# A hybrid state-space and mixture-of-experts layer: scan pairs in another order, low parts made by GpSimd, mixing spread between the last tiles

## The chip, the cores and the metric

One core of one Trainium2 chip runs the whole kernel as one program. The metric is device time in microseconds (us), from three runs. The profile is of one further execution. TensorE (PE in the rows, PEld for its weight loads), VectorE (DVE), ScalarE (ACT), GpSimd (POOL) and SyncE (SP, which only issues DMAs here) each run their own list of instructions in order and wait for one another on semaphores.

## The reference

One decoder layer is computed for 320 tokens (256 of a prompt, 8 samples of 8) with 1024 channels:

```python
hn = rmsnorm(x, norm_mix); proj = hn @ w_in
z, xbc, dt_raw, uv, gates = jnp.split(proj, [...], axis=-1)
conv = conv_b + sum(xpad[:, k:k + l] * conv_w[k] for k in range(4)); xbc_act = silu(conv)
y_ssd, new_ssm = ssd_chunked(xs, dt, a_log, b_ssm, c_ssm, ssm_init)     # the scan: 32 heads of 64, state 128, chunks of 128
y_ssd = rmsnorm((y_ssd + d_skip * xs) * silu(z), gnorm_w)
u, v = split(gelu(uv)); v = layernorm(v); y_mlp = u * (w_spatial @ v + b_spatial)
merged = sigmoid(g_ssd) * (y_ssd @ w_branch_ssd) + sigmoid(g_mlp) * (y_mlp @ w_branch_mlp)
h = x + merged @ w_out
h = h + moe_ffn(rmsnorm(h))                                             # top 4 of 32 experts; then the final rmsnorm
```

## The kernel before

The time has two large parts. Up to about 640 us runs the mixer (projection, scan, branches, output); after it the 32 experts, in pairs, whose weights stream in from memory. The change is in the first 450 us.

**Tiles.** `hn` is turned by TensorE into `hnT` (8 transposes of 3 pieces), and every projection tile is 128 output channels by 320 tokens. Weights and activations are each cut into a high part and a rest ("low part"), so that three products of reduced-precision matmuls make one full product: for a tile `q`, ScalarE casts the weights to the high part (`split_tile` on ScalarE, counted by `split_hi`), VectorE subtracts it from the weights (`split_tile` on VectorE, `split_lo`), and TensorE runs 24 matmuls in two halves of 12 (`half_tile`), lines 827 to 836. The tile that is split is always four ahead of the one just read.

**Stages.** First the `dt` tile and the eight `v` tiles, then four `z` tiles and six `conv` tiles, then the eight mixing products (`mix`, with VectorE's `add_mix_bias` behind each) and the last rows of the convolution state (`last_rows`, read by ScalarE's `read_rows`). Then comes the scan: 16 pairs of heads, `for j in range(PAIRS)` on every engine. Four pairs share a group of the state-space inputs. Beside the scan's own small matmuls each pair `j` carries the two or three projection tiles that `beside(j)` names: three in the first and second pair of a group, two in the third and fourth. In groups 1 to 3 they are six `conv` and four `z` tiles, in the last group `u` tiles and two halves of the gates.

**One pair, before, on TensorE:** `heads` (into PSUM banks 3 and 4), `turn_state` half 0, `diagonal` of the pair before, the first half-tile, in the third and fourth pair of a group `last_rows` (bank 2), `turn_state` half 1, `chunk_states`, `turn_x` of the next pair (bank 2 too), a half-tile, `new_state` and `off_diagonal` half 0, a half-tile, `new_state` and `off_diagonal` half 1, and the last half-tiles. `new_state` half 0 waits for ScalarE's second `read_state`, `new_state` half 1 for VectorE's first `sample_states`, since all use bank 7.

**On the others:** ScalarE reads the heads (`read_heads`, an exponential), copies states (`read_state`), makes `exp(seg)` (`exponent`), reads tiles (`read_beside`) and splits high parts. VectorE runs `segments`, which waits for `read_heads`, then convolutions (`convolve`, six instructions), `gated` (the output of the pair before), `weigh` (operands of the next pair), `sample_states`, and splits low parts. GpSimd multiplies the decays (`decay`), squares the outputs (`squares`) and packs convolution rows (`pack_of`). Each engine's order is the written order; nothing reorders it.

Of the kernel before, what the change touches and what calls it, by code (L numbers as in the profile page):

```python
# [20 lines left out]
P = 128  # L21
# [96 lines left out]
def build(nc, x_prompt, x_sample, state_conv, state_ssm, norm_mix, w_in, conv_w, conv_b, dt_bias, a_log,  # L118
# [4 lines left out]
    with ctx:  # L123
# [352 lines left out]
        MIX_BANKS = (5, 6, 3, 7)  # L476
        BRANCH = ([("mlp", 0), ("w", 2)] + [("y", i) for i in range(4)]
# [106 lines left out]
        def _(pool):  # L584
# [221 lines left out]
        def _(pe):  # L806
# [48 lines left out]
            for k in range(KD):  # L855
                if k >= 4:
                    pe.wait_ge(S["hnT_ready"], k - 3)
                for c in range(3):
                    mm = turn(bank[(2, 3, 6, 7)[k % 4]][:, tok(c)], hn[0:rows(c), c, k * P:k * P + P])
# [27 lines left out]
            for m in range(3, 8):  # L887
                project("v", m)
                turn_v(m - 1)
            project("z", 0)  # L890
# [5 lines left out]

            pe.wait_ge(S["dt_w"], 1)
            for kind, src in enumerate((0, None, 3, 4)):
                for c in range(3 if kind < 3 else 1):
                    v = acumT[0:H, tok(c)] if src is None else dtmp[0:H, src, tok(c)]  # L900
                    mm = turn(bank[4][0:rows(c), kind * 96 + c * H:kind * 96 + c * H + H], v)
            mm.then_inc(S["tm_psum"], 1)
            project("conv", 4)
            project("conv", 5)
# [11 lines left out]
            def last_rows(g, part):  # L916
# [3 lines left out]
                for i in range(count):  # L920
                    mm = turn(bank[2][0:STATE_ROWS, i * P:i * P + P], pack[:, first + i, :])
# [3 lines left out]
            pe.wait_ge(S["ws_ready"], 2)  # L925
            last_rows(0, 0)
            pe.wait_ge(S["v_ready"], 3)
# [4 lines left out]
            for g in range(4, GH):  # L932
                mix(g)

            def gate_half(m, i):
# [5 lines left out]
                if i == 0:  # L941
# [3 lines left out]
                    else:  # L945
                        pe.wait_ge(S["seg_ready"], PAIRS)
# [47 lines left out]
            def heads(j):  # L994

                if j:
                    pe.wait_ge(S["seg_ready"], j)
# [76 lines left out]
            for j in range(PAIRS):  # L1074
# [17 lines left out]
                if j + 1 < PAIRS:  # L1092
                    if jj >= 2 and after_g < G:
# [1462 lines left out]
```

## Time and profile before

| | us |
|---|---|
| median of the three runs (1637.15, 1639.44, 1639.19) | 1639.19 |
| the profiled execution's own time | 1635.9 |
| its span, first to last instruction | 1634.1 |
| TensorE busy in the span | 1492.4 (91%) |
| VectorE, ScalarE, GpSimd busy | 609.4, 372.9, 206.2 |
| the stretch of the 16 scan pairs, 115.9 to 449.2 | 333.3 |

How to read it: a row of the table of stretches gives the stretch, its length, each engine's busy time with its number of instructions, the granted TensorE clock as a share of full speed, the DMA share and GB/s. A timeline row gives start, duration, engine, line, operation, tiles, shape and count, and in brackets how long the engine was idle before it and who ended that. `arena` is one large on-chip buffer that holds most tiles of the mixer; `bank` is PSUM; `ring_r` holds the split weights. Pair `j` starts with its two matmuls of line 1002.

### The profile page before, as it was taken

To read this page: it belongs to the slowest core of one execution; us is meant where nothing else is said; L and a number is where in the kernel's file an instruction comes from. 1 tells how busy PE (TensorE), PEld (TensorE's weight loads), DVE (VectorE), ACT (ScalarE), POOL (GpSimd) and SP (SyncE) were. 2 spreads that over 40 slices of the span, in tenths; PEclk is the share of its full clock that TensorE was granted. 3 is DMA by queue.
4 is the path that set the end of the run, shared out by engine and by line. 5 is a ranking of instruction groups with operands and counts; after the bars stand their busy time and mean duration, and the time that the engine had idled before them with its cause. 6 is when DMAs were issued, how large, how long until landed. Compare 5 with 4: busy or idle time off the path is not lost.

```text
span 1634.1 us, 21958 instructions
## 1 busy us (share of the span) xinstructions
PE 1492.4 (91%) x8487; PEld 877.9 (54%) x8488; DVE 609.4 (37%) x1335; ACT 372.9 (23%) x626; POOL 206.2 (13%) x303
## 2 busy tenths in 40 slices
PE   5999898989999999999999998997899899999986
PEld 4988777878799964443443443443244334434432
DVE  4785676675574414221221221311231212212213
ACT  4554545454353315100100100100011001001002
POOL 4022232323275000000000000000000000000000
PEclk9998988899899999999999999998999999999998
DMA  6532433434354473999999999999699999999994
GB/s 211 155 110 82 125 117 107 135 107 135 100 153 154 155 275 142 429 427 428 429 428 428 428 429 430 427 428 421 277 428 429 430 428 428 429 429 430 428 427 183
DMA packets 123471, 495.85 MB, mean 303 GB/s; under 512 B 7205, under 2 KB 95325, under 8 KB 98009
## 3 DMA queue, kind: packets, MB, share of 16 engines
q1 hardware_dynamic: 85216, 471.74, 71.0%
q10 hardware_dynamic: 35888, 18.88, 4.0%
q0 software_dynamic: 2304, 4.40, 0.9%
q8 instruction: 40, 0.66, 0.2%
q14 instruction: 23, 0.18, 0.0%
HBM read 483.65 MB, written 11.34 MB: 303 GB/s over the span
## 4 chain that ended last, share of the span: by engine, by line
PE 57%; DMA 27%; DVE 7%; issue 5%; ACT 2%; SPq 1%; POOL 1%; ACTq 0%; DVEq 0%; POOLq 0%
DMA ring_b<-in_w_gu 26%; PE bank L1306 16%; PE bank L1359 9%; PE bank L1145 6%; PE bank L827 3%; PE bank L836 3%; PE bank L1259 3%; PE bank L1056 2%; PE bank L1067 2%; PE bank L832 2%; PE bank L1160 2%; PE bank L829 2%; PE bank L808 1%; DVE arena L2131 1%; DMA ring<-in_w_in 1%
## 5 line engine op out<-in xcount | busy, mean ns | idle before, releaser
L1306 PE MATMUL bank<-ring_b,xe 128*64 128x512 f32 x1280 | 353.3, 618 | 43.2 <-DMA ring_b<-in_w_gu 43.2
L1306 PEld LDWEIGHTS bank<-ring_b,xe 128*64 128x64 f32 x1280 | 116.7, 142 | 264.1 <-issue 263.7
L1306 PE MATMUL bank<-ring,xe 128*64 128x512 f32 x768 | 226.0, 594 | 5.7 <-DMA ring<-in_w_gu 5.5
L1359 PE MATMUL bank<-ring,actT 128*64 128x512 f32 x768 | 228.8, 598 | 0.0
L1479 ACT ACTIVATE swi<-swi 128x256 f32<-128x256 f32 x66 | 27.4, 417 | 569.3 <-DVE swi L2352 569.3
L2352 DVE TENSOR_SCALAR swi<-bank 128x256 f32<-128x256 f32 x64 | 27.2, 425 | 340.2 <-PE bank L1306 335.1
L1145 PE MATMUL bank<-rounded,ring_r 128*128 128x320 f32 x912 | 134.3, 308 | 1.9 <-DVE ring_r L2179 1.9
L1145 PEld LDWEIGHTS bank<-rounded,ring_r 128*128 128x128 f32 x912 | 133.2, 188 | 3.1 <-DVE ring_r L2179 2.9
L782 POOL TENSOR_TENSOR kept<-take 128x256 bf16<-128x256 bf16 x15 | 9.2, 613 | 875.7 <-PE bank L1341 875.7
L1359 PE MATMUL bank<-ring_b,actT 128*64 128x512 f32 x256 | 114.5, 601 | 4.3 <-ACT actT L1831 4.3
L1306 PEld LDWEIGHTS bank<-ring,xe 128*64 128x64 f32 x768 | 75.0, 137 | 77.1 <-issue 77.1
L1359 PEld LDWEIGHTS bank<-ring,actT 128*64 128x64 f32 x768 | 69.3, 137 | 63.1 <-issue 62.8
L2370 DVE TENSOR_TENSOR hid<-hid,bank 128x512 f32<-128x512 f32 (+1 forms) x90 | 57.8, 683 | 116.4 <-PE bank L1283 116.4
L827 PE MATMUL bank<-rounded,ring_r 128*128 128x320 f32 x456 | 89.5, 343 | 0.6 <-ACT rounded L1506 0.6
L836 PE MATMUL bank<-rounded,ring_r 128*128 128x320 f32 x456 | 81.4, 323 | 0.0
L1924 DVE TENSOR_TENSOR ring_r<-ring,ring_r 128x1024 fp32r<-128x1024 f32 (+1 forms) x61 | 75.4, 1237 | 3.5 <-ACT ring_r L1499 3.4
L808 PE MATMUL bank<-ident,arena 128*128 128x128 f32 (+7 forms) x305 | 50.9, 288 | 27.8 <-DVE arena L1917 17.4
L827 PEld LDWEIGHTS bank<-rounded,ring_r 128*128 128x128 f32 x456 | 75.3, 208 | 1.8 <-DVE ring_r L1924 0.8
L836 PEld LDWEIGHTS bank<-rounded,ring_r 128*128 128x128 f32 x456 | 74.8, 202 | 0.0
L1359 PEld LDWEIGHTS bank<-ring_b,actT 128*64 128x64 f32 x256 | 34.1, 138 | 66.0 <-issue 65.9
L1499 ACT CAST ring_r<-ring 128x1024 fp32r<-128x1024 f32 (+1 forms) x61 | 63.4, 1040 | 8.2 <-DMA ring<-in_w_in 6.7
L2463 DVE SCALAR_TENSOR_TENSOR ye_lo<-bank,routing,ye_hi 128x512 fp32r<-128x512 f32 x32 | 22.6, 746 | 113.2 <-ACT ye_hi L1842 113.2
(353 smaller groups left out, 2070.2 us busy)
## 6 DMA issues: line engine op xcount, KB each, us to landing
ring_b<-in_w_gu SPq DMA_DIRECT2D x83, 2048.0 KB, 17.1
ring<-in_w_down SPq DMA_DIRECT2D x50, 2048.0 KB, 18.8
ring<-in_w_gu SPq DMA_DIRECT2D x49, 2048.0 KB, 16.8
ring<-in_w_in SPq DMA_DIRECT2D x32, 1024.0 KB, 5.4
ring_b<-in_w_down SPq DMA_DIRECT2D x16, 2048.0 KB, 14.7
arena<-in_state_ssm ACTq DMA_DIRECT2D x16, 512.0 KB, 5.0
out<-arena ACTq DMA_DIRECT2D x16, 512.0 KB, 3.6
ring<-in_w_branch_ssd SPq DMA_DIRECT2D x8, 1024.0 KB, 5.3
```

The costliest lines, as they stand in the source:

```text
L808: return pe.transpose(out, in_, ident[0:in_.shape[0], 0:in_.shape[0]])
L827: pe.matmul(o, w_h[k], hn_hi[:, k, :], start=(k == 0), stop=False)
L829: pe.matmul(o, w_l[k], hn_hi[:, k, :], start=False, stop=False)
L832: pe.matmul(o, w_l[k], hn_hi[:, k, :], start=False, stop=False)
L836: mm = pe.matmul(o, w_h[k], hn_lo[:, k, :], start=False, stop=(k == KD - 1))
L1145: mm = pe.matmul(bank[4 * m + b][:, 0:T], w[:, k, m * P:m * P + P], v[:, k0 + k, :], start=(k == 0 and which != 4 and v is x_h and w is w_ ...
L1259: mm = pe.matmul(bank[6 + k // 4][:, (k % 4) * P:(k % 4) * P + P], part[0:rows(c), c, k * P:k * P + P], chosen_rows[0:rows(c), c, :], star ...
L1306: mm = pe.matmul(bank[q][side(h), :], xe[:, j, side(h)], moe_slot(2 * i + h)[:, 2 * FF * k + 512 * q:2 * FF * k + 512 * q + 512], start=Fa ...
L1359: mm = pe.matmul(bank[4 + half][side(h), :], actT[:, f, side(h)], w[:, D * k + 512 * half:D * k + 512 * half + 512], start=False, stop=(f ...
L1499: act.copy(hi, w).then_inc(S["split_hi"], 1)
L1924: dve.tensor_tensor(lo, w, hi.bitcast(F32), ALU.subtract).then_inc(S["split_lo"], 1)
L2370: dve.tensor_tensor(hid[0:rows(c), c, hb(c, half)], hid[0:rows(c), c, hb(c, half)], bank[6 + i % 2][0:rows(c), :], ALU.add).then_inc(S["cm ...
```

## The change

The scan's order is rewritten on every engine. On TensorE `last_rows` moves behind `turn_x`, into bank 3, and `heads` waits for ScalarE's exponentials (`e_ready`). On VectorE `segments` no longer waits for `read_heads`; on ScalarE `read_heads` waits for `segments`. ScalarE reads the last tile of the pair before first, both `read_state` halves and `read_chunk_states` come ahead of the tiles and of the stores, and casts are separate from tile reads. The low parts of all tiles that are split in the scan (38) are made by GpSimd's new `split_tile`. Ahead of the scan, mixing is put between the last two `conv` tiles, the small transposes that fill `tm` and half of the statistics of `v` move into the `v` tiles, and the transposes of `hn` use six banks, not four, with one split ahead of them, not three.

```diff
 # GpSimd, in the scan
+            def split_tile(q):
+                pool.wait_ge(S["split_hi"], q + 1)
+                pool.wait_ge(S["split_lo"], q)
+                w, hi, lo = tile_of(q)
+                pool.tensor_tensor(lo, w, hi.bitcast(F32), ALU.subtract).then_inc(S["split_lo"], 1)
...
                 decay(j)
                 if j:
                     squares(j - 1)
+                    kind, n = beside(j - 1)[-1]
+                    split_tile(tile_no(kind, n) + 4)
                 for i, n in enumerate(convs):
                     if i:
                         prefix_of(n)
                     pack_of(n)
+                for kind, n in beside(j)[:-1]:
+                    if kind != "gs":
+                        split_tile(tile_no(kind, n) + 4)
 # TensorE
-                if k >= 4:
-                    pe.wait_ge(S["hnT_ready"], k - 3)
+                if k >= 6:
+                    pe.wait_ge(S["hnT_ready"], k - 5)
...
-            for g in range(4):
-                mix(g)
+            mix(0)
+            mix(1)
+            project("conv", 4)
+            mix(2)
+            mix(3)
+            project("conv", 5)
+            last_rows(0, 0)
...
             def heads(j):
                 if j:
-                    pe.wait_ge(S["seg_ready"], j)
+                    pe.wait_ge(S["e_ready"], j)
...
-                elif jj >= 2 and after_g < G:
-                    pe.wait_ge(S["xw_ready"], j + 1)
-                    last_rows(after_g, jj - 2)
...
                 if j + 1 < PAIRS:
-                    if jj >= 2 and after_g < G:
-                        pe.wait_ge(S["cs_ready"], 2 * after_g + jj - 1)
                     turn_x(j + 1)
+                if jj >= 2 and after_g < G:
+                    pe.wait_ge(S["e_ready"], j + 1)
+                    last_rows(after_g, jj - 2)
 # ScalarE
             def read_heads(j):
-                act.wait_ge(S["head_psum"], j + 1)
+                act.wait_ge(S["seg_ready"], j + 1)
...
+                if j:
+                    read_beside(late)
+                    convolved += [n for kind, n in (late,) if kind == "conv"]
+                read_state(j, 0)
                 read_heads(j)
-                read_state(j, 0)
                 exponent(j)
                 if jj == 0:
                     read_b(j // 4)
-                elif jj >= 2 and after_g < G:
+                read_state(j, 1)
+                read_chunk_states(j)
+                if jj >= 2 and after_g < G:
                     read_rows(after_g, jj - 2)
                 if j:
-                    store_states(j - 1)
+                    split_after(late)
 # VectorE
             def segments(j):
                 dve.wait_ge(S["head_psum"], j + 1)
-                dve.wait_ge(S["e_ready"], j + 1)
...
             def use(tile):
-                if kind != "gs":
-                    split_tile(tile_no(kind, n) + 4)
...
                 segments(j)
                 if j:
-                    use(beside(j - 1)[-1])
+                    gated(j - 1)
+                    use(late)
```

GpSimd, from the middle of the second pair of a group (pair 1) to the casts behind the third's decay. Lines 664 and 665 pack rows (663 and 664 in the kernel before), 686 is `decay` (685), 695 to 697 `squares` (694 to 696), 653 the prefix (652). Before:

```order
L663 COPY arena<-arena 128x3
L664 COPY arena<-arena 128x24
L652 COPY arena<-arena 128x8x3
L685 TENSOR_TENSOR arena<-arena 128x640
L694 TENSOR_TENSOR arena<-arena 128x320
L695 TENSOR_TENSOR arena<-arena 128x320
L696 TENSOR_SCALAR arena<-arena 128x320
L663 COPY arena<-arena 128x3
```

and after:

```order
L664 COPY arena<-arena 128x3
L665 COPY arena<-arena 128x24
L716 TENSOR_TENSOR ring_r<-ring,ring_r 128x8x128 x2
L653 COPY arena<-arena 128x8x3
L686 TENSOR_TENSOR arena<-arena 128x640
L695 TENSOR_TENSOR arena<-arena 128x320
L696 TENSOR_TENSOR arena<-arena 128x320
L697 TENSOR_SCALAR arena<-arena 128x320
L716 TENSOR_TENSOR ring_r<-ring,ring_r 128x8x128
L664 COPY arena<-arena 128x3
```

Two subtractions of 128 by 1024 elements now stand between the pack of the second pair's last tile and the third pair's decay, and a third one behind its squares.

ScalarE, the start of pair 2 (the third of its group). Lines 1558 and 1559 (1577 and 1578 after) and the activation of 320 behind them read a `conv` tile, 1499 (1517) is a cast to a high part, 1638 (1658) `read_state`, the 64x192 activations `read_heads`, the 128x640 one `exponent`, 1647 (1667) and 1650 (1670) `read_chunk_states`, 1586 (1606) `read_rows`. Before:

```order
L1499 CAST ring_r<-ring 128x8x128 [waits proj_ready]
L1479 ACT_TABLE_LOAD [waits off_read,sn_ready]
L1479 ACTIVATE arena<-bank 64x192 [waits head_psum]
L1479 ACTIVATE arena<-bank 64x192
L1638 COPY arena<-bank 128x512 [waits off_psum,sT_psum]
L1479 ACTIVATE arena<-arena 128x640 [waits yd_psum,seg_ready]
L1586 COPY arena<-bank 27x512 [waits cs_psum]
...
L1479 ACT_TABLE_LOAD
L1479 ACTIVATE arena<-arena 128x320 [waits conv_done]
L1638 COPY arena<-bank 128x512 [waits off_psum,sT_psum]
```

and after:

```order
L1577 COPY arena<-bank 128x256 [waits packed,conv_act,conv_done,proj_ready]
L1578 COPY arena<-bank 128x8x8
L1497 ACTIVATE arena<-bank,arena 128x320
L1658 COPY arena<-bank 128x512 [waits off_psum,sT_psum]
L1497 ACT_TABLE_LOAD [waits off_read,sn_ready]
L1497 ACTIVATE arena<-bank 64x192 [waits seg_ready]
L1497 ACTIVATE arena<-bank 64x192
L1497 ACTIVATE arena<-arena 128x640 [waits yd_psum,seg_ready]
L1658 COPY arena<-bank 128x512 [waits off_psum,sT_psum]
L1667 COPY arena<-bank 128x128 [waits off_psum,sf_psum]
L1670 COPY arena<-bank 128x128 [waits s_fin_out0]
L1606 COPY arena<-bank 27x512 [waits cs_psum]
```

The second `read_state` now follows the exponential directly; the cast, the row read, the stores and the silu that stood ahead of it are behind it.

## Rows read from the trace of the kernel before

**Rows 1.** Table of stretches: the scan, then pairs 9 to 14.

```profile
115.90:449.20 333.30, 310.70 (x1849) 258.41 (x1848) 208.98 (x527) 159.03 (x287) 103.14 (x133) 0.90 0.37 111
...
313.30:334.60 21.30, 20.24 (x127) 17.51 (x126) 13.26 (x32) 10.53 (x18) 5.68 (x7) 0.92 0.33 103
334.60:352.60 18.00, 15.96 (x106) 12.74 (x105) 13.72 (x37) 10.65 (x20) 5.76 (x10) 1.00 0.41 121
352.60:371.00 18.40, 15.79 (x104) 12.56 (x103) 12.39 (x33) 9.39 (x17) 6.12 (x6) 1.00 0.40 118
371.00:391.30 20.30, 20.09 (x136) 16.93 (x135) 12.91 (x30) 9.90 (x17) 8.59 (x9) 1.00 0.55 164
391.30:418.50 27.20, 24.86 (x126) 21.29 (x125) 12.69 (x29) 9.48 (x15) 5.93 (x4) 0.75 0.29 80
418.50:434.00 15.50, 15.34 (x102) 12.37 (x101) 10.35 (x27) 8.21 (x13) 6.62 (x4) 1.00 0.46 141
```

**Rows 2.** TensorE's waits in the scan: us in total, times, longest.

```profile
PE bank L1056 <- ACT arena L1638: 10.8, 10, 2.3
PE bank L808 <- ACT arena L1586: 3.1, 3, 1.0
PE bank L1056 <- DVE arena L2143: 3.0, 2, 1.5
PE bank L808 <- ACT arena L1638: 2.8, 8, 0.5
PE bank L808 <- ACT arena L1589: 2.5, 3, 0.8
```

**Rows 3.** Timeline of TensorE in pair 10: start, us, then the instructions.

```profile
334.57 0.55 PE L1002 MATMUL bank<-rounded,rounded 64*128 64x320 f32 x2
...
344.62 1.09 PE L1056 MATMUL bank<-arena 32*128 32x512 f32 x2 [0.70 <-ACT arena L1638]
...
348.72 1.12 PE L1056 MATMUL bank<-arena 32*128 32x512 f32 x2
```

**Rows 4.** Timeline of ScalarE in pair 10: the second read of the state.

```profile
343.91 0.57 ACT L1638 COPY arena<-bank 128x512 f32<-128x512 f32 x1
```

**Rows 5.** Timeline of VectorE in pair 10.

```profile
338.68 1.51 DVE L2131 TENSOR_SCALAR arena<-bank,arena 128x128 f32<-128x128 f32 x6 [4.06 <-issue]
...
341.22 1.57 DVE L2042 SCALAR_TENSOR_TENSOR arena<-arena 128x64 f32<-128x64 f32 x1
...
345.93 1.34 DVE L2099 TENSOR_TENSOR arena<-bank,arena 128x256 f32<-128x256 f32 x5
347.19 1.11 DVE L2143 SCALAR_TENSOR_TENSOR arena<-arena,bank 128x128 f32<-128x128 f32 x4
```

**Rows 6.** Line 2042 on VectorE alone: ns minimum, median, maximum, first and last start.

```profile
L2042 DVE SCALAR_TENSOR_TENSOR arena<-arena x54: 269/279/1585, 125.6 to 361.3; 128x64 f32<-128x64 f32 x54
```

**Rows 7.** Lines 685 and 695 on GpSimd alone, the same columns.

```profile
L685 POOL TENSOR_TENSOR arena<-arena x16: 1548/1672/2100, 123.8 to 439.9; 128x640 f32<-128x640 f32 x16
...
L695 POOL TENSOR_TENSOR arena<-arena x15: 858/872/2810, 175.1 to 455.1; 128x320 f32<-128x320 f32 x15
```

**Rows 8.** Groups by line: busy us, mean ns of one, idle before.

```profile
L749 POOL TENSOR_TENSOR arena<-arena,bgu_parts 32x512 f32<-32x512 f32 x4 | 6.7, 1677 | 0.3
```

**Rows 9.** Timeline of TensorE at its start.

```profile
23.10 3.83 PE L808 MATMUL bank<-ident,arena 128*128 128x128 f32 x12 [1.97 <-DVE rounded L1930]
27.55 2.47 PE L827 MATMUL bank<-rounded,ring_r 128*128 128x320 f32 x8 [0.61 <-ACT rounded L1506]
```

**Rows 10.** Timeline of VectorE ahead of the scan.

```profile
103.31 0.38 DVE L2064 MEMSET arena<- 128x384 f32 x1
...
104.59 0.48 DVE L2040 SCALAR_TENSOR_TENSOR arena<-arena 128x256 f32<-128x256 f32 x1 [0.26 <-ACT arena L1479]
...
115.20 0.42 DVE L2076 TENSOR_TENSOR arena<-bank,arena 128x256 f32<-128x256 f32 x1 [0.95 <-PE bank L913]
```

**Rows 11.** The page's DMA issues: operation, count, KB each, us to landing.

```profile
arena<-in_state_ssm ACTq DMA_DIRECT2D x16, 512.0 KB, 5.0
```

More of the change, by code:

```diff
@@ L889, in _ @@
                 turn_v(m - 1)
+                if m == 6:
+                    pe.wait_ge(S["dt_w"], 1)
+                    for kind, src in enumerate((0, None, 3, 4)):
+                        for c in range(3 if kind < 3 else 1):
+                            v = acumT[0:H, tok(c)] if src is None else dtmp[0:H, src, tok(c)]
+                            mm = turn(bank[4][0:rows(c), kind * 96 + c * H:kind * 96 + c * H + H], v)
+                    mm.then_inc(S["tm_psum"], 1)
             project("z", 0)
@@ L895, in _ @@
                 project("conv", n)
[L897 to L904, printed above, removed]
             def mix(g):
@@ L920, in last_rows @@
                 for i in range(count):
-                    mm = turn(bank[2][0:STATE_ROWS, i * P:i * P + P], pack[:, first + i, :])
+                    mm = turn(bank[ROWS_BANK if g else 2][0:STATE_ROWS, i * P:i * P + P], pack[:, first + i, :])
                 mm.then_inc(S["cs_psum"], 1)
@@ L1501, in _ @@
             act.wait_ge(S["ident_ready"], 1)
-            for q in range(3):
-                split_tile(q)
+            split_tile(0)
             for k in range(KD):
                 act.wait_ge(S["hnT_psum"], k + 1)
-                act.copy(hn_hi[:, k, :], bank[(2, 3, 6, 7)[k % 4]][:, 0:T]).then_inc(S["hn_hi_ready"], 1)
+                act.copy(hn_hi[:, k, :], bank[2 + k % 6][:, 0:T]).then_inc(S["hn_hi_ready"], 1)
+            for q in range(1, 3):
+                split_tile(q)
             q = tile_no("dt", 0)
@@ L1680, in read_beside, with split_after @@
                     read_u(n)
+            def split_after(tile):
+                kind, n = tile
                 if kind != "gs":
@@ L2001, in _, with half_stats @@
                               ).then_inc(S["dt_w"], 1)
+            stats = ysum[:, 0:36].rearrange("p (c n) -> p c n", c=3)
+            def half_stats(half):
+                for c in range(3):
+                    r = rows(c)
+                    i = dve.bn_stats(stats[0:r, c, 6 * half:6 * half + 6], vtok[0:r, c, hb(c, half)])
+                link(i)
             for m in range(3, 8):
@@ L2087, in _ @@
             add_mix_bias(1)
+            convolve_beside(4)
+            add_mix_bias(2)
+            add_mix_bias(3)
             convolve_beside(5)
-            for g in range(2, GH):
+            for g in range(4, GH):
                 add_mix_bias(g)
@@ L2182, in _ @@
             for j in range(PAIRS):
-                tiles = beside(j)
+                tiles, late = beside(j), beside(j - 1)[-1] if j else None
                 segments(j)
                 if j:
-                    use(beside(j - 1)[-1])
+                    gated(j - 1)
+                    use(late)
                 if j % 4 == 0:
                     mask_cb(j // 4)
-                if j:
-                    gated(j - 1)
-                if len(tiles) == 3:
-                    use(tiles[0])
                 if j + 1 < PAIRS:
@@ L2195, in _ @@
                 sample_states(j, 0)
-                if len(tiles) == 2:
-                    use(tiles[0])
+                use(tiles[0])
                 sample_states(j, 1)
```

84 lines of the change are left out of this document (46 added, 38 removed).

## The prediction

> **What bounds the kernel now.** I read four views in this order. The table of stretches first: in the 16 scan pairs TensorE is busy 310.7 of 333.3 us, so it idles 22.6, and the granted clock is 0.90 on the mean [rows 1]. VectorE is busy for 209 us of it and GpSimd for 103. So TensorE is the bound, with two losses on top: 22.6 us of idling, and 0.10 x 333.3 = 33 us of lost clock. The rows of the pairs show that these go together: pairs 10, 11, 12 and 14 ran at 1.00, pair 13 with 2.3 us of idling at 0.75 [rows 1]. Then the waits, and who ends them: ScalarE's `read_state` (line 1638) 10.8 + 2.8 us, its `read_rows` (lines 1586 and 1589) 3.1 + 2.5, and VectorE's `sample_states` (line 2143) 3.0 [rows 2]. Then the timelines of pair 10 show why. ScalarE comes to its second `read_state` only at 343.91 [rows 4], 9.3 us after the pair's start at 334.57 [rows 3], since it reads and casts tiles first; and VectorE starts `segments` 4.1 us into the pair, after 4.06 us of idling [rows 5], because `segments` waits for `read_heads`.
>
> The expert part behind 450 us has no changed instruction, and starts as soon as the mixer's last product is there. What is saved or lost ahead of it is saved or lost in full.
>
> **The floor of the scan.** A pair without waits at full clock takes: first of a group 20.3 - 0.2 = 20.1 (pair 12). Second: 21.3 - 1.06 idle (21.3 - 20.24) - 8% of 21.3 for the clock = 18.5 (pair 9). Third 18.0 - 2.04 = 16.0, fourth 18.4 - 2.61 = 15.8 (pairs 10, 11). In the last group the two-tile pairs have no row transposes: 15.5 - 0.2 = 15.3 (pair 14) [rows 1]. Three groups of 70.4 and one of 69.2 make 280.4 us, 53 below the 333.3 of now.
>
> **The start: -2.2.** TensorE waited 1.97 us between the first and the second dozen of transposes, which takes 3.83 and starts at 23.10 [rows 9]. With six banks that wait goes: the second dozen starts at 21.1 and ends at 24.9; one cast and one semaphore later, about 25.4, the first tile starts, where it started at 27.55. What hides the two weight casts moved behind, and their low parts, is that tile's own 24 matmuls (the first 8 take 2.47); were it not there, the 2.2 would be used up.
>
> **Mixing between the tiles: -2.7.** Here VectorE is the bound. The copies into `tm` and its memset stood from 103.31 to 104.33, followed by a wait of 0.26; a wait of 0.95 for TensorE came ahead of the last mixing bias [rows 10]. All go: the copies lie in gaps of the `v` tiles, and the products are there long before VectorE gets to them. That is 1.02 + 0.26 + 0.95 = 2.2; I add 0.5 for a shorter chain behind the statistics, between 0 (a square root on ScalarE hides all of it) and 1.9 (three of six statistics go). TensorE will idle longer ahead of pair 0; that costs only clock.
>
> **What a low part costs on GpSimd.** No row shows it. Nearest rows: 0.86 us for 320 elements, 1.55 to 1.67 for 640 [rows 7], so about 2.5 ns for each further one and 0.87 + 704 x 0.0025 = 2.6 us for 1024. Bounds: 640 elements at 1.548 give 2.4 ns each, 2.5 us; the subtraction of 512 elements at 1677 ns [rows 8] gives 3.3 ns each, 3.35 us. I take 2.6, since the same width of 128 partitions stands in rows 7 and not in rows 8.
>
> **What it costs VectorE.** 341.22 in pair 10: a step of the convolution that takes 0.28 us as a rule took 1.57 [rows 5, 6], just while GpSimd's 1.67 us decay ran. VectorE's instructions with one PSUM input kept their time under GpSimd's load (1.11 and 1.34 in rows 5). So a GpSimd subtraction holds up a VectorE instruction with two on-chip inputs until its end, and such a one goes in between two of GpSimd's. The Trainium skill, SBUF — State Buffer, Who interferes with whom, states this as a lock on a shared port, held for a whole instruction; the trace agrees, with the number above. The GPSIMD Engine Reference, Key points, says that VectorE is about twice as fast for elementwise work; its 2048-element figure, halved, would be 2.25 us, an estimate by which the stalls below would come out some 0.7 us a group smaller. By that page the move is a loss on the engine's side; it is one for the kernel only where GpSimd is waited for.
>
> **Pair 10 after the change**, us from its start. VectorE: `segments` 0.7 to 2.2, for it waits for the heads alone. ScalarE: late tile, `read_state`, table, `read_heads` to 3.7, `exponent` to 4.4, second `read_state` to 5.0. TensorE reaches that wait at 8: the 10.8, the two `read_rows` waits (bank 3 now, read later) and the 2.8 go. But GpSimd does two subtractions first, 1.1 to 3.7 and 4.05 to 6.65, with one of `gated`'s two instructions between and the other behind it, to 7.05. The late convolution follows, six instructions (three times 0.40 + 0.28 at their pitch, 2.0 us), interleaved with decay (1.6), the two squares of 0.7 and 0.9: done at 12.4. `weigh` (1.3) to 13.7 and `sample_states` (1.1) to 14.8. TensorE wants that at 348.72 - 334.57 - 2.04 = 12.1 [rows 1, 3]: a new wait of 2.8 in each third pair. Queued behind `sample_states` on VectorE are the next convolution and the output of the pair, for which TensorE waits only a pair later. In the fourth pair only one subtraction is ahead; the same count ends at 12.3 against 11.9: 0.4. In the first and second pair of a group `sample_states` comes before the convolutions, and TensorE has 20 and 18.5 us: no wait. The last group has no convolutions: none. The low parts themselves are in time, each by 3 us or more in this count. On ScalarE the stores, and with them the load of the state after next, move behind the copies and the cast, to about 8 to 9 us; it lands 5.0 later [rows 11], and is due at the next pair's start, at 16.
>
> Sum: 3 groups x 3.2 = 9.6 us of waits where there were 22.6. Clock: 33 us were lost with 22.6, 1.46 each; by that ratio 14. The scan takes 280.4 + 9.6 + 14 = 304, against 333.3: -29.3. All told -2.2 - 2.7 - 29.3 = -34.2, on 1635.9 of the profiled execution 1601.7. The median stands 3.3 above that execution: **1605 us**. With the bounds of the subtraction (2.5 and 3.35 us, each tenth moves a third pair by 0.2), the clock between nothing and twice the ratio's, and the start, this case spans 1592 to 1622.
>
> **The rivals.**
> *All waits go* (chance 0.14). GpSimd's instructions fall where VectorE has none with two on-chip inputs, or a subtraction takes 2.3. For it speaks that VectorE ends only 3.0 us of today's waits, in two places [rows 2]. Against it: VectorE and GpSimd already collide at 341.22. The scan is then 280 to 285: 1635.9 + 3.3 - 4.9 - 51 = about 1583.
> *The wait changes hands* (0.22). With subtractions of 3.35 us and every collision, `sample_states` comes 1.5 later in each third pair, 1 to 2 us late in each other one: 7 us a group, 21 in all with 31 of clock. The scan stays at 333, and 4.9 of the front remain: 1634, which is half within what can be told.
> *The port saturates* (slower, 0.14). The exclusive work of a group is GpSimd's four decays, eight squares, one mask (some 17 us), ten subtractions, and VectorE's six convolutions and eight steps of `gated` (16). With 2.6 us that is 59 of 70.4; with 3.7 it is the whole floor, and from about 4 on GpSimd sets the pair's time. At 10 us of waits a group: 280.4 + 30 + 44 = 354, and 1655. It decides from some 7.5 us of waits a group, a subtraction of about 3.5.
> That the change does nothing is excluded: the rows' waits have their causes in an order that is no longer there.
>
> **How the numbers follow.** Forecast 0.50, all gone 0.14, changed hands 0.22, saturated 0.14. A measurement of this kernel can tell 0.2% (3.3 us) from no change. Faster by more: 0.50 + 0.14 + half of 0.22 = 0.75. Within: 0.10. Slower: 0.15. The range leaves out half of the case in which all waits go (0.07, below 1584) and most of the saturated one (0.12, above 1637): 1584 to 1637. The forecast's own range is 1592 to 1622.
>
> **What would show it.** Right: the first tile near 25.4; pair 0 near 111; no wait left on `read_rows` or the second `read_state`; the wait of `new_state` on `sample_states` up, only in third pairs and of 2 to 3.5 us; subtractions of 2.5 to 2.9 us; convolution steps as long as those where they meet. Wrong: subtractions over 3.3, waits of a half-tile for the low part, waits in first and second pairs, or a clock as low as before in spite of fewer waits.

## The result, and the profile after

The changed kernel takes 1583.43 us (median of four runs, 1583.14 to 1589.26), the kernel before 1638.17 in the same comparison: a ratio of 0.968, 95% interval 0.965 to 0.971. That is faster by 3.2%. The forecast of 1605 us was 21.6 us too slow; the time came out where the rival "all waits go" had put it (1583). It lies outside the forecast's own range of 1592 to 1622 and right at the lower edge, 1584, of the wide one. One execution of run 6 below (1666.0 us) fell in a slower state of the core and is left out of its numbers. The profiled execution took 1583.14 us, with a span of 1581.4 where it was 1634.1.

The table of stretches of the changed kernel, in the columns of [rows 1]: ahead of the scan, the scan, the rest, and then, of a second table, pairs 1 to 4, 6, 7, 10 and 11.

```profile
0.00:112.24 112.24, 92.43 (x609) 86.16 (x610) 79.37 (x161) 59.12 (x97) 26.86 (x67) 1.00 0.57 174
112.24:396.43 284.19, 279.81 (x1847) 235.36 (x1847) 186.16 (x489) 163.22 (x288) 179.66 (x171) 0.98 0.44 130
396.43:1581.40 1184.97, 1088.63 (x6033) 533.06 (x6032) 320.41 (x648) 153.40 (x242) 75.22 (x103) 0.98 0.89 371
...
130.97:149.59 18.62, 18.62 (x127) 15.92 (x126) 10.27 (x34) 10.62 (x18) 8.97 (x13) 1.00 0.41 122
149.59:166.59 17.00, 15.61 (x107) 12.83 (x106) 16.00 (x35) 10.95 (x20) 13.22 (x13) 1.00 0.43 127
166.59:181.91 15.32, 15.32 (x105) 12.62 (x104) 11.63 (x29) 10.06 (x18) 11.98 (x10) 1.00 0.49 143
181.91:201.70 19.79, 19.79 (x136) 16.92 (x135) 13.29 (x33) 11.72 (x22) 13.04 (x13) 1.00 0.58 164
...
220.31:239.65 19.34, 17.85 (x106) 14.94 (x106) 15.69 (x35) 10.94 (x20) 12.91 (x13) 0.87 0.37 113
239.65:255.75 16.10, 16.10 (x104) 13.10 (x103) 10.26 (x29) 10.05 (x18) 11.98 (x10) 0.94 0.45 135
...
294.19:312.49 18.30, 16.80 (x106) 13.88 (x106) 15.70 (x35) 10.95 (x20) 12.93 (x13) 0.93 0.40 119
312.49:328.13 15.64, 15.64 (x104) 12.81 (x103) 11.04 (x29) 10.05 (x18) 11.82 (x9) 0.98 0.48 139
```

The scan took 333.3 us [rows 1] and takes 284.2; the scan began at 115.9 and begins at 112.2. What follows it is as long as before, 1184.97 against 1634.1 - 449.2 = 1184.9. So -3.7 and -49.1 make the whole -52.7, and what is saved ahead of the experts is saved in full, as forecast. In the scan TensorE's idling fell from 22.6 to 4.4 us, and all of it stands in the third pairs of the first three groups (17.00 - 15.61, 19.34 - 17.85 and 18.30 - 16.80). Clock is lost only in pairs 6 and 10 and in the pair behind each; pair 2 keeps 1.00 in spite of its wait: 0.13 x 19.34 + 0.06 x 16.10 + 0.07 x 18.30 + 0.02 x 15.64 = 5.1 us, where 33 were lost. GpSimd is busy for 180 us of the stretch, not 103.

TensorE's waits in the first 450 us of the changed kernel, in the columns of [rows 2]; left out are the 17.3 us ahead of its first instruction and two of 0.6 and 1.0 us outside the scan:

```profile
PE bank L1076 <- DVE arena L2183: 4.4, 3, 1.5
PE bank L1163 <- DVE ring_r L2218: 1.6, 2, 0.8
PE bank L1022 <- DVE arena L2118: 1.2, 1, 1.2
...
PE bank L821 <- ACT arena L1606: 0.6, 1, 0.6
```

Four of the five waits of [rows 2] are gone from the scan, and one is there in a new size: `new_state` on `sample_states` (line 2183 now), once in each of three third pairs. The wait of 1.2 is the one for the last mixing bias ahead of pair 0, the 1.6 are in the branch work behind the scan, and the 0.6 on `read_rows` (line 1606) stands at 108.33, ahead of the scan.

The timeline of the changed kernel in pair 2, a third pair, which began at 149.59: VectorE, then GpSimd's part of it (a second view), then TensorE and ScalarE.

```profile
150.17 1.51 DVE L2171 TENSOR_SCALAR arena<-bank,arena 128x128 f32<-128x128 f32 x6 [1.66 <-PE bank L1022]
...
152.20 1.01 DVE L2201 TENSOR_TENSOR arena<-arena 128x192 f32<-128x192 f32 x1
153.24 2.62 DVE L2203 TENSOR_TENSOR arena<-arena 128x320 f32<-128x320 f32 x1
155.78 0.48 DVE L2086 SCALAR_TENSOR_TENSOR arena<-arena 128x256 f32<-128x256 f32 x1
156.18 1.58 DVE L2088 SCALAR_TENSOR_TENSOR arena<-arena 128x64 f32<-128x64 f32 x1
...
159.88 0.47 DVE L2088 SCALAR_TENSOR_TENSOR arena<-arena 128x64 f32<-128x64 f32 x1
160.27 1.33 DVE L2140 TENSOR_TENSOR arena<-bank,arena 128x256 f32<-128x256 f32 x5
161.53 1.10 DVE L2183 SCALAR_TENSOR_TENSOR arena<-arena,bank 128x128 f32<-128x128 f32 x4
```

```profile
150.60 4.91 POOL L716 TENSOR_TENSOR ring_r<-ring,ring_r 128x1024 fp32r<-128x1024 f32 x2
...
155.88 1.79 POOL L686 TENSOR_TENSOR arena<-arena 128x640 f32<-128x640 f32 x1
...
159.45 1.38 POOL L697 TENSOR_SCALAR arena<-arena 128x320 f32<-128x320 f32 x1
```

```profile
162.69 1.12 PE L1076 MATMUL bank<-arena 32*128 32x512 f32 x2 [1.40 <-DVE arena L2183]
```

```profile
154.10 0.59 ACT L1658 COPY arena<-bank 128x512 f32<-128x512 f32 x1
```

`segments` starts 0.6 us into the pair, where it started after 4.1 in pair 10 of the kernel before [rows 3, 5], and the second `read_state` 4.5 us in, where it came after 9.3 [rows 3, 4]. The two low parts run from 150.60 to 155.51, and `gated`'s last product, usually 0.49 us, takes 2.62: it ends at 155.86, just after the second low part. Its neighbour takes 1.01 in place of 0.36. Then the convolution collides with the decay (156.18, 1.58 us for a step of 0.29), and `sample_states` is done at 162.63, 1.3 us after TensorE first wanted it (162.69 - 1.40 = 161.29). This is the mechanism that the forecast described, with the same instructions in the same places.

### The profile page after: what moved, and what is told of

The parts are those of the page before. It is cut to its first block, busy times and chain, and to the rows that moved or that the text cites. A ratio compares the mean times of both kernels' runs of the same rounds, so it can differ in the third digit from the quotient of the medians.

```text
span 1581.4 us, 22023 instructions
## 1 busy us (share of the span) xinstructions
PE 1460.9 (92%) x8487; PEld 854.6 (54%) x8488; DVE 585.9 (37%) x1297; ACT 375.7 (24%) x626; POOL 281.7 (18%) x341
## 4 chain that ended last, share of the span: by engine, by line
PE 61%; DMA 27%; DVE 7%; issue 2%; ACT 1%; SPq 1%; POOL 1%; DVEq 0%; ACTq 0%; POOLq 0%
DMA ring_b<-in_w_gu 27%; PE bank L1324 17%; PE bank L1377 9%; PE bank L1163 7%; PE bank L849 3%; PE bank L840 3%; PE bank L1277 3%; PE bank L821 3%; PE bank L1076 2%; PE bank L1178 2%; PE bank L845 2%; PE bank L1087 2%; PE bank L842 2%; PE bank L1433 1%; DVE arena L2088 1%
## 5 line engine op out<-in xcount | busy, mean ns | idle before, releaser
L1163 PE MATMUL bank<-rounded,ring_r 128*128 128x320 f32 x912 | 134.3, 308 | 1.8 <-DVE ring_r L2218 1.8
L1163 PEld LDWEIGHTS bank<-rounded,ring_r 128*128 128x128 f32 x912 | 133.2, 187 | 3.0 <-DVE ring_r L2218 2.8
L716 POOL TENSOR_TENSOR ring_r<-ring,ring_r 128x1024 fp32r<-128x1024 f32 x38 | 90.6, 2385 | 2.6 <-ACT ring_r L1517 0.6
L840 PE MATMUL bank<-rounded,ring_r 128*128 128x320 f32 x456 | 81.8, 322 | 0.6 <-ACT rounded L1523 0.6
L849 PE MATMUL bank<-rounded,ring_r 128*128 128x320 f32 x456 | 78.2, 314 | 0.0
L849 PEld LDWEIGHTS bank<-rounded,ring_r 128*128 128x128 f32 x456 | 71.4, 193 | 0.0
L840 PEld LDWEIGHTS bank<-rounded,ring_r 128*128 128x128 f32 x456 | 68.5, 191 | 2.0 <-issue 0.8
L821 PE MATMUL bank<-ident,arena 128*128 128x128 f32 (+7 forms) x305 | 48.4, 283 | 17.9 <-DVE arena L1943 17.3
```

Of the source, the lines that this page charges most:

```text
L716: pool.tensor_tensor(lo, w, hi.bitcast(F32), ALU.subtract).then_inc(S["split_lo"], 1)
L821: return pe.transpose(out, in_, ident[0:in_.shape[0], 0:in_.shape[0]])
L840: pe.matmul(o, w_h[k], hn_hi[:, k, :], start=(k == 0), stop=False)
L849: mm = pe.matmul(o, w_h[k], hn_lo[:, k, :], start=False, stop=(k == KD - 1))
L1163: mm = pe.matmul(bank[4 * m + b][:, 0:T], w[:, k, m * P:m * P + P], v[:, k0 + k, :], start=(k == 0 and which != 4 and v is x_h and w is w_ ...
```

## The experiments

All were timed in three rounds, the last two in five. The kernel before stood at 1635.5 us beside runs 1 to 4 and at 1636.3 us beside the others; ratios are to it. The changed kernel was timed only in the comparison above, beside 1638.2 us, so a difference of 2 or 3 us from its 1583.4 is no more than the kernel before moved from one comparison to the next, and smaller readings rest on the spans and the wait rows. Diffs are against the changed kernel, where nothing else is said.

**1. The low parts a pair earlier.** In each second pair GpSimd makes the low parts at once, before it waits for the convolution's halves that belong to the next pair, so that the third pair starts without them.

```diff
+                if j % 4 == 1 and convs:
+                    for kind, n in beside(j)[:-1]:
+                        if kind == "conv":
+                            pack_of(n)
+                        split_tile(tile_no(kind, n) + 4)
+                    prefix_of(convs[-1])
+                    pack_of(convs[-1])
+                    continue
```

> The changed kernel, but in the second pair of each group GpSimd makes the low parts of its first two tiles before it waits for the last tile's rows, not behind them. My theory: the three waits left in the third pairs (1.40, 1.49, 1.50 us) come from those two subtractions, since they stand at the start of the third pair and hold up the last step of gated (2.62 us where 0.49 is usual) and with it the convolution ahead of sample_states. Then the waits go, and with them the clock lost there (5 us): 9 us less than the changed kernel, near 1574. Rival: the decay and squares alone hold up the convolution enough; then a wait of 1 us or more stays in the third pairs, and the time is within 3 us of 1583. A second rival: the subtractions now collide with the convolution at the end of the second pair and make segments late: waits in new places.

Measured: 1573.7 us, ratio to before 0.962 (0.956 to 0.968), span 1572.1. The timeline of VectorE around pair 2:

```profile
148.37 2.35 DVE L2094 SCALAR_TENSOR_TENSOR arena<-arena 128x256 f32<-128x256 f32 x1
...
152.26 1.50 DVE L2179 TENSOR_SCALAR arena<-bank,arena 128x128 f32<-128x128 f32 x6
...
154.26 0.36 DVE L2209 TENSOR_TENSOR arena<-arena 128x192 f32<-128x192 f32 x1
154.65 0.49 DVE L2211 TENSOR_TENSOR arena<-arena 128x320 f32<-128x320 f32 x1
```

and of GpSimd:

```profile
148.03 2.40 POOL L716 TENSOR_TENSOR ring_r<-ring,ring_r 128x1024 fp32r<-128x1024 f32 x1 [1.07 <-ACT ring_r L1525]
```

The stall went with the subtraction: the products of `gated` are back at 0.36 and 0.49, and a convolution step at the end of pair 1 now takes 2.35 us, about as long as the subtraction beside it. `segments` starts 2.1 us later for it (152.26 in place of 150.17), and TensorE does not come to wait. No wait of `new_state` is left in the scan. The span fell by 9.3, about the 4.4 us of waits and the 5.1 of clock together. Only the place of these subtractions on GpSimd differs, so the stall's cause is shown.

**2. The low parts on VectorE again**, in the rest of the new order: GpSimd's calls are gone, and VectorE makes each behind work of its own that TensorE waits for.

```diff
                 sample_states(j, 0)
+                if j:
+                    low_of_next(late)
                 use(tiles[0])
...
                 decayed(j)
+                low_of_next(tiles[0])
```

> The changed kernel, but with the 38 low parts of the scan on VectorE (1.22 us each), each placed where its high part is there. My theory: GpSimd's share in the gain is nothing, the new order did it all: VectorE has 98 of 284 us free and the port is less used, so the waits in the third pairs vanish and the time is 1574 to 1584. Rival: VectorE needs the relief; then TensorE waits for sample_states or for the low parts in first and second pairs, over 8 us in all, and the time is 1590 to 1610.

Measured: 1572.6 us, 0.961 (0.955 to 0.967), span 1571.4. The stretch from 112 to 397 us, in the columns of [rows 1]:

```profile
112.00:397.00 285.00, 284.95 (x1920) 241.18 (x1921) 210.38 (x533) 171.77 (x295) 97.11 (x136) 1.00 0.45 135
```

TensorE idles for 0.05 us in it, at full clock, though VectorE carries 210 us of work. In this order GpSimd's part in the change brings nothing and costs about 10 us.

**3. Only the low parts moved:** the kernel before, with GpSimd's `split_tile` in the changed kernel's places and none in VectorE's `use`.

```diff
+                    kind, n = beside(j - 1)[-1]
+                    split_tile(tile_no(kind, n) + 4)
...
+                for kind, n in beside(j)[:-1]:
+                    if kind != "gs":
+                        split_tile(tile_no(kind, n) + 4)
```

> The kernel before, with only the 38 low parts moved to GpSimd. My theory: the waits of before were ScalarE's order; they stay (16 to 20 us on read_state and read_rows), and the clock stays near 0.90 in the scan: 1625 to 1650, within 0.8 percent of 1638. Rival: freeing VectorE was worth a good part of the 55 us: 1600 to 1620.

Measured: 1634.4 us, 1.001 (0.997 to 1.005). TensorE's waits in the scan:

```profile
PE bank L1068 <- ACT arena L1650: 13.4, 10, 2.7
PE bank L1068 <- DVE arena L2155: 4.7, 2, 2.4
PE bank L820 <- ACT arena L1598: 3.1, 3, 1.0
PE bank L820 <- ACT arena L1650: 2.8, 8, 0.5
PE bank L820 <- ACT arena L1601: 2.4, 3, 0.8
```

They are the five of [rows 2], 22.2 us there and 26.4 here: a relief of VectorE by 38 low parts removes none of them. With run 2 this shows that the scan's gain is the order's: the order without the move has all of it, the move without the order none.

**4. `segments` waits for the heads' readings again**, as before the change (ScalarE's own wait goes back to TensorE's heads, and TensorE's three waits on `e_ready`, not shown, to `seg_ready`).

```diff
-                act.wait_ge(S["seg_ready"], j + 1)
+                act.wait_ge(S["head_psum"], j + 1)
...
                 dve.wait_ge(S["head_psum"], j + 1)
+                dve.wait_ge(S["e_ready"], j + 1)
```

> The changed kernel, but segments waits for read_heads again, and read_heads for the heads alone, as before. My theory: VectorE starts each pair about 3 us later; in third pairs the wait on sample_states grows from 1.5 to 2 to 4 us each, elsewhere it is covered (TensorE has 3 us or more there): 3 to 8 us more waits, 6 to 15 us slower than 1583. Rival: VectorE's later start is hidden everywhere since GpSimd's two subtractions set the time in third pairs: within 3 us of 1583.

Measured: 1624.7 us, 0.992 (0.990 to 0.995), so 41 us of the change's gain are gone, where 6 to 15 had been expected. TensorE's waits, and VectorE in pair 2:

```profile
PE bank L1076 <- DVE arena L2184: 22.6, 6, 4.3
PE bank L821 <- DVE arena L2184: 2.0, 2, 1.0
```

```profile
154.78 1.51 DVE L2172 TENSOR_SCALAR arena<-bank,arena 128x128 f32<-128x128 f32 x6 [4.90 <-issue]
```

VectorE idles for 4.90 us and comes that much later to `sample_states`: 2.9 to 4.3 us of waiting in each third and fourth pair of the first three groups, and a clock of 0.91 in the stretch from 112 to 397. This run does not tell how much of it is the late start alone, and how much GpSimd's subtractions add to it; run 5 asks that.

**5. The same with the low parts on VectorE** (the edits of 2 and 4).

> segments waits for read_heads again, as in the run that cost 41 us, but the 38 low parts are made by VectorE. It asks what made that wait dear. Theory 1: the late start of VectorE alone puts sample_states behind the convolution in third and fourth pairs; VectorE has 1.2 us more to do for each tile here, so TensorE waits as much as there, 4 us a pair: 1610 to 1625. Theory 2: the late start was dear because it pushed VectorE's two-input steps under GpSimd's subtractions, decay and squares; without the 38 subtractions the waits shrink to 1 to 2 us a third pair: 1578 to 1595.

Measured: 1602.7 us, 0.980 (0.974 to 0.986). Its waits:

```profile
PE bank L1071 <- DVE arena L2179: 12.2, 6, 2.1
```

Against run 2 the late start costs 30 us (12.2 of waits, the rest clock and small waits); with GpSimd's subtractions added it costs 41 against the changed kernel, and the subtractions cost 22 here (4 against 5), where they cost 10 in the changed kernel. The two causes are not independent: both eat the same slack ahead of `sample_states`, and neither of the two ranges that were expected for this run (1610 to 1625, 1578 to 1595) was met.

**6. The second `read_state` late:** it and the chunk states are read by ScalarE behind the stores and the silus, and behind the first tile where there are three, much as before the change.

```diff
-                read_state(j, 1)
-                read_chunk_states(j)
...
                     split_after(tiles[0])
+                read_state(j, 1)
+                read_chunk_states(j)
                 read_beside(tiles[-2])
```

> The changed kernel, but ScalarE reads the second half of the states (and the chunk states) behind the first tile, the stores and the silus again. My theory: this was the largest wait of before (10.8 us with 2.8 more), so the wait of new_state on this copy is back, 1 to 3 us in most pairs, 12 to 30 us in all, with the clock: 1605 to 1640. Rival: with segments early and the casts behind, ScalarE gets there in time anyway, and the time is within 5 us of 1583.

Measured: 1643.3 us, the median of executions of 1638.7, 1643.3 and 1654.4; those of the kernel before beside it took 1627.5 to 1639.5. The expected 1605 to 1640 was passed, and the gain is gone; whether the kernel is slower than the one before, these few executions do not tell. Its span is 1636.9, against 1634.1. ScalarE in pair 2 (which starts at 152.42 here), then TensorE's waits, then the scan's row:

```profile
163.21 0.47 ACT L1497 ACTIVATE arena<-arena 128x320 f32<-128x320 f32 x1 [1.50 <-DVE arena L2088]
163.58 0.57 ACT L1658 COPY arena<-bank 128x512 f32<-128x512 f32 x1
```

```profile
PE bank L1076 <- ACT arena L1658: 22.8, 11, 4.3
```

```profile
112.93:454.27 341.34, 318.30 (x1848) 264.97 (x1848) 185.23 (x489) 161.40 (x288) 178.75 (x171) 0.86 0.37 108
```

The copy stands 11.2 us into the pair, later than the 9.3 of the kernel before, behind an activation that waits for the convolution (line 2088), which GpSimd's subtractions have held up. TensorE waits 22.8 us for it, as much as it idled in all before, and the clock is lower (0.86). So without this place in ScalarE's order the other edits bring nothing in this version. But the run does not price the place alone: part of its 60 us may be the subtractions' doing, and the same edit with the low parts on VectorE was not run. Nor do the parts add up: this run gives back 60 us and run 4 gives back 41, of a gain of 55.

**7. The rows of the convolution state as before** (bank 2, `last_rows` ahead of `turn_state` half 1, `read_rows` right behind `exponent`).

```diff
-        ROWS_BANK = 3
+        ROWS_BANK = 2
...
+                elif jj >= 2 and after_g < G:
+                    pe.wait_ge(S["xw_ready"], j + 1)
+                    last_rows(after_g, jj - 2)
```

> The changed kernel, but with the last rows of the convolution in bank 2 and ahead of turn_x again, read right behind exponent. My theory: the two waits of about 1 us on read_rows come back in third and fourth pairs of three groups, 5 to 6 us, and 3 to 8 of clock: 1589 to 1598. Rival: ScalarE is now early enough there: within 3 us of 1583.

Measured: 1585.8 us, 0.971 (0.967 to 0.975), span 1580.0 (the changed kernel's 1581.4). The waits on `read_rows` do not come back. Both kernels' intervals overlap, so the move of the rows is worth nothing that can be told here (5 to 6 us of waits had been expected back): what made TensorE wait on `read_rows` before was how late ScalarE was, not the bank.

**8. The start as before** (four banks for the turned `hn`, three splits ahead of it).

```diff
-                    mm = turn(bank[2 + k % 6][:, tok(c)], hn[0:rows(c), c, k * P:k * P + P])
+                    mm = turn(bank[(2, 3, 6, 7)[k % 4]][:, tok(c)], hn[0:rows(c), c, k * P:k * P + P])
...
-            split_tile(0)
+            for q in range(3):
+                split_tile(q)
```

> The changed kernel with the transposes of hn on four banks and three splits ahead of them, as before. Both theories: 2.2 to 2.4 us slower, 1585.5; if the scan is bound by something else than its start, less than that.

Measured: 1588.0 us, 0.971 (0.968 to 0.975). Medians cannot part it from the changed kernel; the span is 3.5 us longer (1584.9), one profiled execution each. TensorE's timeline at the start of the changed kernel, to read beside [rows 9]:

```profile
17.30 7.35 PE L821 MATMUL bank<-ident,arena 128*128 128x128 f32 x24 [17.30 <-DVE arena L1943]
25.26 2.47 PE L840 MATMUL bank<-rounded,ring_r 128*128 128x320 f32 x8 [0.61 <-ACT rounded L1523]
```

All 24 transposes run in one piece, and the first tile starts 2.29 us earlier than in [rows 9].

**9. GpSimd's work behind each low part raised** by three additions of 320 elements (3.0 to 3.1 us together; their results are not used).

```diff
+                for i in range(3):
+                    link(pool.tensor_tensor(sq, hn_hi[:, i, :].bitcast(F32), hn_hi[:, i + 3, :].bitcast(F32), ALU.add))
```

> The changed kernel with three further additions of 320 elements on GpSimd behind each of the 38 low parts (about 2.6 us more each; their result is not used). This prices the saturated port of the prediction: the two engines' exclusive work then comes to some 80 us a group of which TensorE needs 69. My theory: TensorE waits 7 to 15 us a group for sample_states and low parts and the kernel gets close to before or over it, 1620 to 1660. Rival: the lock holds up less than a whole instruction (the convolution of a third pair took 4.5 us where I had counted 5.4), and the load is hidden: 1590 to 1610.

Measured: 1617.5 us, 0.990 (0.986 to 0.993). Its waits:

```profile
PE bank L1078 <- DVE arena L2185: 13.0, 5, 3.6
PE bank L1165 <- POOL ring_r L716: 4.1, 1, 4.1
PE bank L1078 <- ACT arena L1660: 3.0, 2, 1.5
```

GpSimd is busy for 251 of the 285 us behind 112. Even so 13.0 of these 20.1 us are waits for VectorE, held up beside it, and only once, right behind the scan, does TensorE wait for a low part itself. With 2.3 times GpSimd's work for a low part the kernel loses 34 us and stays ahead of the one before; both ranges that were expected (1620 to 1660, 1590 to 1610) missed it. The saturated rival had put 1655 us at a subtraction of about 3.5 us. Here GpSimd has 5.4 us of two-input work for each low part, and the time is 1617.5: that rival counted the two engines' work as dearer than it is.

**10. The low parts only written:** two fills with zero in place of each subtraction, 1.9 us together. They read nothing; the low parts are left out of the products' values.

```diff
-                pool.tensor_tensor(lo, w, hi.bitcast(F32), ALU.subtract).then_inc(S["split_lo"], 1)
+                link(pool.memset(lo.bitcast(F32), 0.0))
+                pool.memset(lo.bitcast(F32), 0.0).then_inc(S["split_lo"], 1)
```

> The changed kernel, but in place of each of the 38 subtractions GpSimd writes zeros into the low part, twice, which takes about as long and reads nothing on chip. (It leaves the low parts of those weights out.) Lock on the reading side, as the Trainium skill has it (SBUF, Who interferes with whom): VectorE's two-input steps keep their 0.28 to 0.49 us during it, the step of gated in third pairs falls from 2.62 to 0.5 us, the three waits on sample_states go, and the time is 1572 to 1577. If any GpSimd instruction blocks VectorE: the steps stay at 1.5 to 2.6 us, the waits stay, and the time is 1581 to 1586.

Measured: 1573.0 us, 0.962 (0.956 to 0.968). VectorE's product of `gated`, and GpSimd beside it:

```profile
151.84 0.49 DVE L2204 TENSOR_TENSOR arena<-arena 128x320 f32<-128x320 f32 x1
```

```profile
151.91 0.96 POOL L716 MEMSET ring_r<- 128x1024 f32 x1
```

Both run at once and the product keeps its 0.49 us, where it took 2.62 beside a subtraction. So it is not GpSimd's being busy, nor its writing, that holds VectorE, but that its instruction reads on-chip operands.

**11 and 12. The two best orders again,** in five rounds: runs 1 and 2 as they were.

> The same kernel as in the run with GpSimd's low parts early in the second pair (1573.7 us), in more rounds, beside the one with the low parts on VectorE. My theory: 1573, as the other; if the shared load costs anything that the wait rows don't show: 2 us or more above it.

> The same kernel as in the run with the low parts on VectorE (1572.6 us), in more rounds: to tell it from the kernel in which GpSimd makes them early. My theory: neither has a wait in the scan that is left, so both take 1573 and the ratio between them is 1 within 0.2 percent. If VectorE's load matters anywhere: over 1577.

Measured: low parts a pair earlier 1574.3 us (1572.6 to 1576.3), 0.963 (0.958 to 0.967); on VectorE 1572.8 us (1571.8 to 1573.7), 0.962 (0.957 to 0.966). Both are about 10 us faster than the changed kernel. The ratios to the kernel before do not part them from its 0.968 (0.965 to 0.971), since that kernel itself scatters by over 20 us; the times do: no execution of these two orders took over 1576.7 us, and none of the changed kernel's under 1583.1. Between the two the medians differ by 1.4 us, 0.1%, too little to choose by; VectorE's version leaves GpSimd out of it.

## Why the prediction was right, and where it was off

- **What bounds it, and the chain.** Right. TensorE is the bound, the waits on `read_state` and `read_rows` had their cause in the engines' order (runs 2 and 3), and without the early `read_state` nothing is gained (run 6). Of the two reasons given for `read_rows`, the other bank was not one (run 7). What lies behind the scan kept its length.
- **The start: -2.2.** Right: -2.29, the first tile at 25.26 where 25.4 was forecast.
- **Mixing: -2.7.** Mis-sized. Of the 3.7 us ahead of the scan, 1.4 are left beside the start's. The wait of 0.95 for TensorE did go, but VectorE's list was not shorter by its whole length: VectorE has no idle time from 99.5 us on, and TensorE waits for it ahead of pair 0 (1.2 us, `L1022 <- DVE L2118`). Pair 0 starts at 112.2, not near 111. Undoing the mixing alone was not run, so the 1.4 is a difference of two readings.
- **The low part: 2.6 us.** It takes 2.39 (median of 38, 2.35 to 2.46), below the lower bound of 2.5. The line through 320 and 640 elements [rows 7] was too steep.
- **What it costs VectorE.** Right in kind: 2.62 us for a product of 0.49 and 1.01 for one of 0.36, gone when the subtraction is moved (run 1), taken off (run 2) or replaced by a write (run 10). The Trainium skill, SBUF — State Buffer, Who interferes with whom, states an exclusive lock that lasts for the whole instruction; these runs agree for GpSimd's two-input instructions, but not for its one-input operation (last section). The Trainium skill, GPSIMD Engine Reference, Elementwise — side-by-side cycle accounting, has 4497 ns for 2048 elements; half of it, 2.25 us, was an estimate for the subtraction, nearer to the 2.39 than mine. The prediction took the move for a loss only where GpSimd is waited for. That was wrong: it costs 10 us here while TensorE never waits for GpSimd in the scan, because it waits for VectorE, which GpSimd holds.
- **Pair 10 after the change: `sample_states` at 14.8, wanted at 12.1.** I had it 1.8 us too late: read in pair 2, it ends 13.0 us into the pair. Of this 0.8 had arisen when `gated` ends (6.3 in place of 7.05: shorter subtractions, and an earlier start), and 0.9 in the convolution (4.5 us, counted at 5.35). TensorE came for it at 11.7. The wait is 1.4 to 1.5, in place of 2.8; in the fourth pair there is none, in place of 0.4. So 4.4 us of waits, where 9.6 were forecast: 5.2 of the miss. The terms named for the convolution (2.0, 1.6, 0.7 and 0.9) make 5.2, not the 5.35 between 7.05 and 12.4.
- **Clock: 14 us.** The biggest miss: 5.1 were lost, 9 less. 7.6 of these follow from fewer waits at the same 1.46 (5.2 x 1.46); the rest, 1.3, from a lower price, 1.16 us for each us of wait. So the waits' size is at the root of nearly 13 of the 21.6 us. Pair 2 idled 1.40 us and kept 1.00, pair 6 idled 1.49 and fell to 0.87: a ratio taken from 22.6 us of waits is rough for three short ones. The rows had shown it: pairs 10 and 11 idled 2.04 and 2.61 us at 1.00 [rows 1], against the prediction's sentence that the two losses go together.
- **The floor: 280.4 us.** It is 284.2 - 4.4 - 5.1 = 274.7. A third pair is 15.6 without its wait and a fourth 15.3, where I had 16.0 and 15.8, second pair and first 18.6 and 19.8; pair 0, which carries no output of a pair before, takes 18.7. This is 5.7 of the miss. I took an undisturbed pair from pairs with waits, less their idle time, and that leaves a rest in: without a wait TensorE's next instructions start, by the rows, some 0.16 us before the last have ended (170.38 + 0.60 and 170.82 in pair 3 after the change), and ahead of a wait this overlap is lost and counted as busy. Pair 11 had three waits and 15.79 us of busy time [rows 1]; pair 3 after the change, also a fourth pair and without a wait, has 15.32.
- **The base.** I added 3.3 us to get from the profiled execution to the median. The kernel after shows 0.3 between the two: 3 of the miss.

The sum, then: 5.2 + 9 + 5.7 + 3 - 1.2 (ahead of the scan) = 21.7 of the 21.6. The mechanism held, and the sizes did not: of three signs set down for the forecast, the wait was 1.4 to 1.5 us and not 2 to 3.5, the subtraction 2.39 and not 2.5 to 2.9, and pair 0 came at 112.2. Nearly all sizes in the scan erred to the long side (the second pair alone was 0.1 short), so the misses added up instead of cancelling, and took the time out of the forecast's own range. The rival "all waits go" met the number, but not the way: three waits remained, and the lower floor and the smaller step to the median made up for them. That this rival's number was met is luck. "The wait changes hands" and "the port saturates" did not happen (the latter's 17 us of GpSimd's work a group are also 14 by the rows: 6.7 of decays, 6.4 of squares, 1.0 of the mask); run 9 shows that even 2.3 times the work for a low part does not bring the second about.

What stays open: how the change's parts would rank if each were undone in the best version (runs 1 and 2), what the mixing's move is worth by itself, and what the late second `read_state` costs when VectorE makes the low parts.

## What to carry to other kernels

When one engine waits for many results in a fixed order, order each helper's list by when that engine needs them: one 0.6 us copy left behind stores and silus cost 60 us here, while taking 38 instructions off the busiest helper brought nothing. Try such moves together: two of them each gave back most of the gain when undone alone. Before work is given to GpSimd, look at which VectorE instructions with on-chip operands run beside it and who waits for those; it is free only in the pairs that have slack. Count a TensorE wait at more than its length, and take the size of an undisturbed stage from a stage that shows neither waits nor a lowered clock.

## What the runs showed of the hardware

- **The clock's price of a wait varies.** All kernels in the scan: 22.6 us of idling with 33 lost before, 4.4 with 5.1 after, and in run 6 23.0 us (341.34 - 318.30) with 0.14 x 341.34 = 48. Idling cost between 1.2 and 2.1 us of clock for each us, by clock shares that the rows give to 0.01.
- **A fill does not hold up VectorE; a subtraction does.** 0.49 us under a fill of 1024 elements, 2.62 under a subtraction of the same tile. GpSimd's one-input operation of line 697 does not hold VectorE for its length either: VectorE's step at 159.88 took 0.47 beside it, not the 1.38 of GpSimd's, and in pairs 6 and 10 (230.18, 304.08) a step of 0.48 took 0.78. It can also be VectorE that holds GpSimd: in the kernel before, where this operation is line 696 and takes 1.09 us at its shortest, it took 2.52 beside VectorE's own subtraction, which kept its 1.21 (no run was made for that one alone):

```profile
195.62 2.52 POOL L696 TENSOR_SCALAR arena<-arena 128x320 f32<-128x320 f32 x1
...
195.97 1.21 DVE L1924 TENSOR_TENSOR ring_r<-ring,ring_r 128x1024 fp32r<-128x1024 f32 x1
```

- **GpSimd's exclusive instructions and VectorE's take turns.** Two subtractions in a row let one instruction of VectorE in between them (152.20, held to the end of the first subtraction, then 153.24, held to the end of the second).
